# One layer of a hybrid decoder on one core: four units of y_a W_a computed inside the odd turns of the delta rule instead of in the merge

## The reference

```python
x = x + 0.5 * swiglu(rmsnorm(x, n_f1), f1_g, f1_u, f1_d)
h = rmsnorm(x, n_mix)
proj = h @ w_in
sc_b, sc_c, sc_x, qkv_pre, a_raw, b_raw, z, gate_a, gate_b = split_columns(proj)
y_a = sc_b * causal_dwconv(sc_c * sc_x, sc_buf, sc_w)
y_b, gdn_s = gdn_mixer(qkv_pre, a_raw, b_raw, z, ...)      # chunked delta rule, 8 heads
merged = sigmoid(gate_a) * (y_a @ w_a) + sigmoid(gate_b) * (y_b @ w_b)
x = x + merged @ w_o
x = x + 0.5 * swiglu(rmsnorm(x, n_f2), f2_g, f2_u, f2_d)
```

## Time and profile before

| what | value |
|---|---|
| median of the runs | 3455.48 us |
| span of the profiled execution | 3453.9 us |
| TensorE busy | 3322.5 us (96%), 20286 matmuls |
| VectorE, ScalarE, GpSimd busy | 1326.3, 1013.5, 891.1 us |
| mean granted TensorE clock | 0.975 of full |
| DMA | 222.74 MB, mean 64 GB/s |

### The profile page before, as it was taken

One profiled execution on the slowest core, in us unless ns is written; L12 is line 12 of the kernel. 1 busy time (PEld: TensorE's weight loads), 2 busy tenths in 40 slices (PEclk: granted clock), 3 DMA queues, 4 the chain that ended last, 5 costly groups with the idle time before them and its releaser, 6 DMA issues. The chain is left out here.

```text
span 3453.9 us, 51790 instructions
## 1 busy us (share of the span) xinstructions
PE 3322.5 (96%) x20286; PEld 3236.0 (94%) x20286; DVE 1326.3 (38%) x2186; ACT 1013.5 (29%) x1408; POOL 891.1 (26%) x506
## 2 busy tenths in 40 slices
PE   8999999998999799999999999879999999999998
PEld 8999999998999699899999998769999999999998
DVE  4333333334777433333333333333223333333333
ACT  5111111114222354444444454321024111111113
POOL 2121121214122333323333333212233121111112
PEclk9999999999999899999999999779999999999998
DMA  4111111112222212112112121354312111111111
GB/s 135 40 49 43 43 43 43 43 43 79 73 86 88 81 51 69 58 51 68 58 51 75 51 69 36 99 195 151 120 38 74 43 43 49 43 43 43 36 30 52
DMA packets 274431, 222.74 MB, mean 64 GB/s; under 512 B 12042, under 2 KB 251786, under 8 KB 274288
## 3 DMA queue, kind: packets, MB, share of 16 engines
q1 hardware_dynamic: 273988, 220.56, 21.0%
q10 hardware_dynamic: 324, 0.41, 0.0%
HBM read 170.66 MB, written 50.28 MB: 64 GB/s over the span
## 5 line engine op out<-in xcount | busy, mean ns | idle before, releaser
L209 PE MATMUL ffn_bank<-ffn_h_hi,ffn_w_hi 128*128 128x368 f32 x2112 | 698.2, 331 | 6.8 <-DVE ffn_h_lo L618 6.8
L210 PE MATMUL ffn_bank<-ffn_h_lo,ffn_w_hi 128*128 128x368 f32 x2112 | 699.2, 331 | 0.0
L211 PE MATMUL ffn_bank<-ffn_h_hi,ffn_w_lo 128*128 128x368 f32 x2112 | 697.9, 330 | 0.0
L209 PE MATMUL mix_bank<-mix_h_hi,mix_w_hi 128*128 128x368 f32 x1752 | 639.5, 365 | 6.6 <-DVE mix_pre L1750 3.2
L408 POOL TENSOR_TENSOR ffn_w_lo<-g_w_raw,ffn_w_hi 128x1024 fp32r<-128x1024 f32 x130 | 310.9, 2400 | 1191.4 <-ACT ffn_w_hi L404 1191.3
L210 PE MATMUL mix_bank<-mix_h_lo,mix_w_hi 128*128 128x368 f32 x1752 | 580.3, 331 | 0.0
L211 PE MATMUL mix_bank<-mix_h_hi,mix_w_lo 128*128 128x368 f32 x1752 | 579.0, 330 | 0.0
L209 PEld LDWEIGHTS ffn_bank<-ffn_h_hi,ffn_w_hi 128*128 128x128 f32 x2112 | 398.3, 189 | 8.1 <-issue 8.0
L211 PEld LDWEIGHTS ffn_bank<-ffn_h_hi,ffn_w_lo 128*128 128x128 f32 x2112 | 398.0, 188 | 0.0
L210 PEld LDWEIGHTS ffn_bank<-ffn_h_lo,ffn_w_hi 128*128 128x128 f32 x2112 | 397.8, 188 | 0.1
L817 POOL TENSOR_TENSOR mix_w_lo<-g_w_raw,mix_w_hi 128x1024 fp32r<-128x1024 f32 x73 | 186.0, 2549 | 782.0 <-ACT mix_w_hi L812 782.0
(11 more groups left out here) (242 smaller groups left out, 4559.5 us busy)
## 6 DMA issues: line engine op xcount, KB each, us to landing
g_w_raw<-in_w_in SPq DMA_DIRECT2D x73, 512.0 KB, 6.0
g_w_raw<-in_ffn_w_gate SPq DMA_DIRECT2D x44, 512.0 KB, 3.8
g_w_raw<-in_ffn_w_up SPq DMA_DIRECT2D x44, 512.0 KB, 3.8
g_w_raw<-in_ffn_w_down SPq DMA_DIRECT2D x44, 512.0 KB, 3.5
scratch_qkv<-mix_out SPq DMA_DIRECT2D x24, 552.0 KB, 2.8
turn_kq<-scratch_qkv SPq DMA_DIRECT2D x32, 256.0 KB, 3.9
scratch_x<-g_x SPq DMA_DIRECT2D x8, 552.0 KB, 7.2
scratch_z<-turn_z_out SPq DMA_DIRECT2D x8, 552.0 KB, 2.8
```

The lines of the kernel that those rows point to most:

```text
L209: pe.matmul(out, w_hi, x_hi, start=first, stop=False)
L210: pe.matmul(out, w_hi, x_lo, start=False, stop=False)
L211: return pe.matmul(out, w_lo, x_hi, start=False, stop=last)
```

## The change

The last full turn takes all 36 pieces and the split of the next weights (`TURN_ORDER` in place of `LAST_ORDER`), so that all of `h @ w_in` is done when it ends. SyncE then loads y_a over the place of h_lo, ScalarE copies each chunk over h_hi and VectorE subtracts in place. The odd turns carry units 0 to 3 of y_a W_a, 44 pieces, 22 a turn: eight of 9 matmuls (one chunk of the contraction for all three thirds, each with its own wait for its y_a chunk), then 36 of 6. Their results are multiplied with sigmoid(gate_a), which is loaded back from memory, and stored to `merged_a`. The merge starts with units 4 to 7 of y_a W_a on the h_hi and h_lo that the mixer leaves, its loads of z and y_b are interleaved, and `merged_a` is loaded back during the round. The number of dense matmuls is the same before and after.

The diff, cut to its core:

```diff
-LAST_ORDER = [(name, k) for name, k in TURN_ORDER if k < {"dense": 12, "evict": 3}.get(name, 99)]
+WA = NQ + 3 * TURNS
+WA_UNITS = 4
+WA_PIECES = KC + 12 * (WA_UNITS - 1)

 def odd_order(g):
-    order, piece = [], [12 * (g + 1)]
+    order, piece = [], [0 if g == 0 else WA_PIECES // 2]

     def dense(count):
         for _ in range(count):
-            order.append(("dense", piece[0]))
-            if piece[0] % 4 == 3:
-                order.append(("evict", piece[0] // 4))
+            n = piece[0]
+            if n < KC:
+                order.append(("ya_split", n))
+            order.append(("wa", n))
+            if n == KC - 1:
+                for b in range(NB):
+                    order.append(("wa_evict", b))
+                order.append(("wa_split", NB))
+            elif n >= KC and (n - KC) % 4 == 3:
+                order.append(("wa_evict", NB + (n - KC) // 4))
             piece[0] += 1

     order.append(("load", 0))
-    dense(1)
+    if g:
+        dense(1)
     order.append(("kk", 0))
     order.append(("lu", 0))
-    dense(1)
+    if g:
+        dense(1)
     order.append(("qk", 0))
     order.append(("kt", 0))
+    dense(1)
     order.append(("zero", 0))
     order.append(("square", 0))
     dense(1)
@@ for k in range(1, TAIL_LEVELS)
         order.append(("X", k))
         dense(1)
         order.append(("T", k))
+        if g or k > 1:
+            dense(1)
     order.append(("sk", 0))
+    dense(2)
     order.append(("turn", 0))
-    dense(1)
+    dense(2)
     order.append(("nu", 0))
-    dense(1)
+    dense(2)
     order.append(("oo", 0))
     for k in range(HG):
         order.append(("ds", k))
+        if k % 2:
+            dense(1)
         if k == 1:
-            dense(1)
             order.append(("scale", 0))
     order.append(("os", 0))
+    dense(WA_PIECES // 2 * (g + 1) - piece[0])
     order.append(("out", 0))
@@ SyncE, step and odd_step
                 elif name == "evict" and g == 1 and (k in (2, 5) or k == 8 and isinstance(i, int)):
+                    if k == 8:
+                        sp.wait_ge(w.unit_done, NB * WA)
+                        sp.wait_ge(ya_stored, 16 * (1 + KC))
+                        for c in range(KC):
+                            sp.dma_start(h_lo[:, c, :].bitcast(F32), scratch["y_a"][c]).then_inc(ya_in[c], 16)
                     store_gate(k // 3, i)
...
+                if name == "wa_evict" and k % NB == NB - 1:
+                    u = k // NB
+                    for b in range(NB):
+                        sp.wait_ge(bank_free[b], WA + u + 2)
+                    sp.dma_start(scratch["merged_a"][u], gate_out[1 + u % 2][:, :]).then_inc(wa_stored[u % 2], 16)
+                elif name == "zero" and d.g == 0:
+                    for u in range(2):
+                        load_sig(u)
@@ TensorE, odd_step
+                if name == "wa":
+                    if k < KC:
+                        if k == 0:
+                            w.wait(pe, 0, 3, WA)
+                            for b in range(NB):
+                                pe.wait_ge(bank_free[b], WA + 1)
+                        pe.wait_ge(ya_lo, k + 1)
+                        for b in range(NB):
+                            mm = thirds_pass(WA, b, k, WA % 3)
...
@@ ScalarE, odd_step
+                if name == "wa_split":
+                    w.split_hi(act, 0, 3, WA + k)
+                elif name == "ya_split":
+                    act.wait_ge(ya_in[k], 16)
+                    act.copy(h_hi[:, k, :], h_lo[:, k, :].bitcast(F32)).then_inc(ya_hi, 1)
@@ VectorE, odd_step
+                if name == "ya_split":
+                    dve.wait_ge(ya_hi, k + 1)
+                    dve.tensor_tensor(h_lo[:, k, :], h_lo[:, k, :].bitcast(F32), h_hi[:, k, :].bitcast(F32), ALU.subtract).then_inc(ya_lo, 1)
+                elif name == "wa_evict":
+                    j, b = divmod(k, NB)
+                    if b == 0:
+                        dve.wait_ge(wa_sig[j % 2], 16 * (j // 2 + 1))
+                    dve.wait_ge(w.unit_done, NB * (WA + j) + b + 1)
+                    buf = gate_out[1 + j % 2][:, third(b)]
+                    dve.tensor_tensor(buf, bank[b][:, 0:TH], buf, ALU.mult).then_inc(bank_free[b], 1)
@@ merge_outputs, SyncE
-            for c in range(KC):
-                sp.dma_start(x[:, c, :], scratch["y_a"][c]).then_inc(ya_loaded[c], 16)
             slots.take_over(sp, w.raw_loaded)
-            gates(0, 0, 0)
+            for c in range(2):
+                load_z(c)
+                load_yb(c)
+            for j in range(2):
+                gate(0, 0, 0, j)
...
+            for c in range(WA_UNITS):
+                sp.dma_start(merged[:, c, :], scratch["merged_a"][c]).then_inc(ma_loaded, 16)
@@ merge_outputs, VectorE
+            for n in range(FIRST):
+                j = n % 2
+                gate_yb(2 * n)
+                dve.wait_ge(sig_loaded[j], 16 * (n // 2 + 1))
+                for b in range(NB):
+                    dve.wait_ge(unit_done, NB * n + b + 1)
+                    dve.tensor_tensor(merged[:, WA_UNITS + n, third(b)], bank[3 * j + b][:, 0:TH], sig[:, j, third(b)], ALU.mult) \
+                        .then_inc(bank_free[3 * j + b], 1)
+                    if b == 1:
+                        gate_yb(2 * n + 1)
```

More of the change, by code:

```diff
@@ L1279, in odd_step @@
                             .then_inc(d.v_loaded if j == 2 else d.qk_loaded, 16)
-                    if d.g:
+                    if d.g == 0:
+                        for n in range(3):
+                            w.load(sp, 0, 3, WA + n, block_cols(w_a, n * P))
+                    else:
+                        w.load(sp, 0, 3, WA + 3, block_cols(w_a, 3 * P))
                         sp.wait_ge(ya_stored, 16 * (1 + KC))
@@ L1299, in _ @@
                 sp.wait_ge(st_stored[k], 64)
-            sp.wait_ge(w.lo_done, NQ + 3 * TURNS)
+            for k in range(2):
+                sp.wait_ge(wa_stored[k], 16 * (WA_UNITS // 2))
+            sp.wait_ge(w.lo_done, WA + WA_UNITS)
             slots.load_ahead(sp, ahead)
@@ L1974, in _ @@
         def _(sp):
-            def loads(r, i):
-                for j in range(2):
[L1977 to L1983, removed]
@@ L1985, in _, with weight @@
-            for c in range(KC):
-                sp.dma_start(x[:, c, :], scratch["y_a"][c]).then_inc(ya_loaded[c], 16)
-            slots.take_over(sp, w.raw_loaded)
-            gates(0, 0, 0)
[L1989 to L1992, removed]
-                sp.dma_start(x[:, c, :], scratch["z"][c]).then_inc(z_loaded, 16)
-            for r in range(3):
+            def weight(r, i, n, j):
+                w.load(sp, i, 2, at[r] + n + j, weights[r][:, bass.ds(i * (2 * P) + (n + j) * P, P)].rearrange("(k p) n -> p k n", p=P))
@@ new lines, in gate, with load_z, load_yb @@
+            def gate(r, i, n, j):
+                sp.wait_ge(sig_used, i * 2 + (at[r] + n + j + 1))
+                first = WA_UNITS if r == 0 else 0
+                sp.dma_start(sig[:, j, :], scratch["sig_a" if r == 0 else "sig_b"][bass.ds(i * 2 + (first + n + j), 1)]
+                             .rearrange("c p t -> p (c t)")).then_inc(sig_loaded[j], 16)
+            def load_z(c):
+                sp.dma_start(x[:, c, :], scratch["z"][c]).then_inc(z_loaded[c], 16)
+            def load_yb(c):
+                if c >= 2:
+                    sp.wait_ge(y_gated, c - 1)
+                sp.dma_start(y_raw[:, c % 2, :], scratch["y_b"][c]).then_inc(y_loaded[c % 2], 16)
@@ new lines, in _ @@
+            slots.take_over(sp, w.raw_loaded)
+            for c in range(2):
[3 more added lines that the diff above has]
+                gate(0, 0, 0, j)
+            w.load(sp, 0, 2, 2, block_cols(w_a, (WA_UNITS + 2) * P))
+            for c in range(2, 5):
+                load_z(c)
+                load_yb(c)
+            w.load(sp, 0, 2, 3, block_cols(w_a, (WA_UNITS + 3) * P))
+            gate(0, 0, 2, 0)
+            for c in range(5, KC):
+                load_z(c)
+                load_yb(c)
@@ new lines, in _ @@
+            gate(0, 0, 2, 1)
+            for c in range(WA_UNITS):
+                sp.dma_start(merged[:, c, :], scratch["merged_a"][c]).then_inc(ma_loaded, 16)
+            for r in range(1, 3):
+                for j in range(2):
+                    weight(r, 0, 0, j)
+                if r == 1:
+                    for j in range(2):
+                        gate(1, 0, 0, j)
+                    for c in range(KC):
+                        sp.wait_ge(y_ready, c + 1)
+                        sp.dma_start(x[:, c, :], scratch["x"][c]).then_inc(x_loaded, 16)
@@ L2004, in _ @@
[L2004 to L2013 removed]
+                            gate(1, i, 2, j)
+            sp.wait_ge(w.lo_done, at[2] + KC)
```

201 lines of the change are left out of this document (114 added, 87 removed).

## The result

The changed kernel takes **3464.83 us** (median of 7 runs), the kernel before 3455.2 beside it on the same chip: ratio **1.0028, 95% interval 1.0018 to 1.0037**, so 6 to 13 us slower. The forecast was 3458.2 in a range of 3446 to 3470: the time lies in the range, but on the side of the first rival (the split pieces keep the clock down, 3464.4), and the change is slower by 0.28%, more than the 0.2% that the prediction called the least that can be told from none. The profiled execution has a span of 3461.3 us against 3453.9, 7.4 more; it took 3463.13, 1.7 under the median.

The account below looks back on a forecast made before the run. TensorE was taken to bound the kernel nearly everywhere, except a 285.6 us stretch with close to 80 us of waits or lower clock. Terms +10.1 +39.6 +6.1 +1.4 +0.6 -4.0 -49.8 -1.3 = +2.7 gave 3458.2 us, range 3446 to 3470.

Parts of the forecast that it names:

- the first rival: First odd turn: gaps before eight pieces hold the lower clock until seg, stage 64.7 us, kernel 3464.4; chance 0.36.
- Last full turn: Kk to kk: 53.5 to 63.6 us, +10.1 for 24 more pieces, 4.6 of it a new wait behind ScalarE's Ln.
- First odd turn, kk to seg: Stage from 18.9 to 58.5 us, +39.6, the middle of 52.1 at full clock and 64.7 at the lower.
- Piece 1: First odd turn: second split piece, behind squares waiting for q and k queued after y_a, put at 16.0 us after kk.
- The rival that had q and k in time: First odd turn: q and k land 3 us after issue; with a high clock stage 46.8 us, kernel 3446.5; chance 0.18.
- The state parts: Odd turns after seg: first, to next kk, 39.2 to 45.3 us (+6.1); second, to os, 33.7 to 34.3 (+0.6).
- the second odd turn's levels: Second odd turn, kk to seg: 17.1 to 18.5 us, +1.4, with four more pieces.
- the 14.7 from os to the merge: From os to the merge's first dense matmul: 18.7 to 14.7 us, -4.0.
- The merge: First round: 100.7 to 50.9 us, -49.8, for 288 matmuls plus tails, clock and waits, with its loads just hidden.
- the turnover: After the merge's first round: 3.8 to 2.5 us, -1.3, as VectorE has no product with z before the first y_lo.
- The text's 2.8 for meetings with GpSimd: Odd turn: GpSimd's masks may meet the new VectorE subtractions twice, 2 x 1.4 us, kept for the range, 0 in the sum.
- The third rival: First odd turn: both copies hidden and TensorE waits for none, stage some 27 us, kernel 3426; chance 0.04.

Follow-up runs that it names:

- Experiment 5: On top of experiment 3, ScalarE takes the norm's Ln and Exp ahead of the gate's sigmoid and the weights' split in the last full turn; 3431.26 us (one execution).
- fillers: Changed kernel plus 90 more matmuls in TensorE's waits before pieces 1 to 7 of the first unit, nothing moved; 3449.98 us (one execution).
- the second pair: Kernel with 90 more matmuls in its waits and the unedited changed kernel, both run again on the same chip; 3452.09 us and 3465.2 us.
- experiment 3: Both edits on the changed kernel: y_a's copies and subtractions one piece earlier, and q, k, v loaded ahead of y_a; 3430.05 us, ratio 0.9927.
- Experiment 2: Changed kernel with SyncE issuing the second odd turn's q, k and v ahead of the y_a loads; 3458.35 us, ratio 1.0003 to the kernel before.
- experiments 1: Changed kernel with each copy and subtraction of y_a one piece earlier in the written order; 3435.78 us, ratio 0.9939 to the kernel before.
- 4: Changed kernel without the ScalarE copy and VectorE subtraction of y_a, each piece waiting only for its own load; 3433.61 us (one execution).
- Experiment 6: On top of experiment 3, w_b's first weights are loaded after the sixth z and y_b in the merge; 3425.37 us (one execution).

## Why the prediction came out as it did

**Last full turn: right.** 63.28 against 63.6, with the new wait before kk at 4.51 (4.6 forecast), released by ScalarE's Ln. Experiment 5 confirms the queue ahead of it as its cause.

**First odd turn, kk to seg: the step that failed.** The places were right: eight waits, VectorE named in each. Two terms of the sum were off.
- *The clock.* The text had 52.1 at the full clock and 64.7 at the lower, asked "which holds?" and took the middle, 58.5. The granted clock was 0.62, near the low end, and the stage 65.3, over the 63 that the text had named as the sign of a wrong clock. The argument was two old stretches, one high (10.0 us, TensorE busy 6.6) and one low (16.4, busy 13.1), and that the new one was "as gappy as either". It was gappier than both (busy 38.2 of 65.3), and neither stretch stood at a middle. Laid out on TensorE's timeline, the seven pieces from piece 1 on take 18.3 us, where the text had 10.5 at the full clock and 8.9 more at the lower, and what lies between them 29.3, where it had 25.7 and 3.7 more: 11.4 of the distance of 12.6 came, 6.3 was booked. The experiments agree: at least 9.3 (fillers), 12.0 (the second pair), 12.3 of busy time (both edits). The first rival had this as its mechanism, with 0.36 against 0.42 for the forecast.
- *Piece 1.* 16.0 after kk was forecast, 17.7 measured. The prediction's own two figures don't fit each other: squares let go "some 15 us after kk" and piece 1 at 16.0 leave 1.0 for squares, copy and subtraction, which took 3.2 (the squares start at 14.5, the piece at 17.7). From the first issue of y_a to the squares 19.0 us pass, and the bytes at 330 GB/s gave 17. Left out were the store that waits 2.2 for VectorE's `turn_o` and the 5.93 that the issue takes; how the 2.0 divides among them and the rate stays open. Experiment 2 shows what standing behind all of this, loads and store together, is worth: 6.2 us of the stage. The rival that had q and k in time (3446.5) was rightly doubted for the order of the queue, but it also promised a high clock from it, and that didn't come: 0.58 with q and k in time. Only the kernels that take the waits away (experiments 1, 3, 4 and those built on 3) or fill them (7) have 0.78 or more.

That the rival's 64.7 lies 0.6 from the measured 65.3 is in part luck: piece 1 came 1.7 later than it had, and what followed took 47.6 and not 48.8. Its 3464.4 beside 3464.83 owes as much to parts it hadn't priced (below).

**The state parts: too long, 2.3 and 1.7.** 43.0 and 32.6 against 45.3 and 34.3. The states' chain on VectorE was put on TensorE's path with a start of its own; with TensorE busy 42.0 of 43.0, it is wholly hidden. (Its old length was misread as well: from nu_seg at 2217.60 to os at 2233.44 it is 15.8, not 15.3; read rightly the forecast would have been 0.5 further off.) The clock of these stages also rose, from 0.67 to 0.80 and from 0.72 to 0.84. The 18.5 of the second odd turn's levels and the 14.7 from os to the merge were right within 0.4.

**The merge: 3.2 too short.** 51.98 us for the dense work and the tails against 50.9, and the turnover 4.59 against 2.5. I had taken the product with z off VectorE's path, and it did leave; but before, GpSimd's split of round 1's first weights ran from 2400.87 for 2.40 us and was over 3.3 us ahead of the turnover at 2406.6, and now their load stands behind the gates and the four units. So ScalarE's copy starts behind a split, and VectorE's first subtraction meets GpSimd. The change moved a DMA of another purpose in the queue, and that step was not costed. Experiment 6 gives the 2.5 forecast once this is put right. The text's 2.8 for meetings with GpSimd was kept in the range for the masks in the odd turn. There, too, the first subtraction took 1.77 instead of 1.30, 0.5 us; the real one was elsewhere.

**The sum.** +2.7 was forecast, +7.9 measured up to round 1. The 5.2 between them are +6.8 for the first odd turn, -2.3 and -1.7 for the state parts, +3.2 for the merge, and -0.8 in small things. So errors of both signs cancelled in part; without the shorter ones the time would have stood at some 3470, at the very edge of the range. That it lies well inside is luck.

**The third rival** (both copies hidden, 3426, chance 0.04) is what the two edits of experiment 3 make of the change: 3430. I had written "only with both engines a level ahead could it be, and they are not". That was right for this kernel, and it also named the repair.

## What to carry to other kernels

- Moving work into idle time pays only if its inputs are ready before the slot: an input that is prepared "just before use" in an order written out by hand stands behind the step it should overlap. Emit the preparation one slot earlier; here that turned +0.3% into -0.6%, and -0.9% with the loads of q, k, v and w_b's weights put right.
- Where a stage can stand at either clock level, price it at both. Where no stretch of the trace is like it, nothing says which holds: keep each as an outcome with its own time and chance, and don't book the mean: here it booked 6.3 us for the clock, and 11.4 came.
- When loads are added to a queue, go through what now stands behind them, whatever it serves, and through the waits among them.

## What the runs showed of the hardware

Here work that isn't needed paid for itself through TensorE's clock: 90 matmuls put into waits raised the granted clock from 0.62 to 0.89 (0.54 to 0.91 in the second pair) and made the kernel 13 us faster. The Trainium skill (TensorE: Matmul & The Clock Gate, What's actually happening) says that the default state is throttled and activity releases it; the traces agree, with 9.3 to 12.0 us for this one stage. That is about the whole difference between the kernels before and after (7.4 in the spans, 9.6 in the medians).

The issue of a load itself took long on a loaded queue: q and k took 5.93 us from the first issue to the end of the second behind y_a, and the same two 1.14 us ahead of it (timeline of SyncE, experiment 3):

```profile
2183.30 1.14 SPq L1296 DMA_DIRECT2D turn_kq<-scratch_qkv  x2
```

So what SyncE has to issue next is late by that too. How it divides between the queue's room and the engines' share was not tried.
